# Moving SBUF tile addresses: an arena on a 128-byte boundary, feature tiles 1040 and 1088 bytes apart

## The chip, the cores and the metric

The kernel runs on one core of one Trainium2 chip. The metric is the device time of one execution in microseconds (us), given as the median of several executions. SBUF is the on-chip memory with 128 partitions; an address here is a byte offset within a partition, and it is the same in all 128.

## The reference

The program takes 256 tokens of width 1024 through two networks in float32.

The first has two layers. A layer is a SwiGLU feed-forward (`x += 0.5 * (silu(h @ w_gate) * (h @ w_up)) @ w_down`, hidden width 2816), a mixer (a projection of width about 7300, a gated spatial unit, an RWKV-7 recurrence over time, two gated projections and an output projection), and another SwiGLU feed-forward.

The second has two layers over the tokens and, in its first layer, over 256 context tokens as well: RMS norm with a scale and shift from a conditioning vector, attention (differential in the first layer, neighbourhood attention with a bias in the second), and a feed-forward with a three-tap convolution over positions between its up- and down-projection (hidden width 2816). A last RMS norm gives the output.

What bears on the change is only this: nearly all the arithmetic is products `h @ W`, where `h` has 256 rows and `W` is a large weight matrix.

## The kernel before

**Products.** A product is done in float32r, a 4-byte format of less precision. To come near float32 each operand is split in two: a high part (rounded to float32r) and a low part (the rest). Three matmuls replace one: high x high, high feature x low weight, low feature x high weight.

The weights are the moving operand. They come from HBM as a stream of 371 units of 128 x 2048 float32 (1 MB). SyncE loads a unit into `raw` (2 slots), ScalarE writes `w_hi` (line 1147, 4 slots), VectorE subtracts and writes `w_lo` (line 1668, 4 slots), and TensorE reads both. The features are the stationary operand, stored by feature: a tile `[128, KT, T]` holds K tiles of 256 tokens, and one weight load takes 128 of the tokens, 512 bytes in every partition. `HA_hi`/`HA_lo` are the main feature tiles (8 K tiles each); `HB_hi`/`HB_lo` hold a second stream or the recurrence's output (8 K tiles); `FT_hi`/`FT_lo` hold the hidden features of the feed-forwards (22 K tiles).

`block_wide` multiplies one feature tile set with two units. Its inner part is `unit_wide`; each `mm` is one weight load and one matmul of 512 columns, both recorded at line 481:

```
for k in range(4):
    for t in range(tiles):
        a  = h_hi[:, 4 * part + k, P * t:P * t + P]
        al = h_lo[:, 4 * part + k, P * t:P * t + P]
        mm(acc[:, t, 0:width], a,  w_hi[:, s, cols_], ...)
        mm(acc[:, t, 0:width], a,  w_lo[:, s, cols_], ...)
        mm(acc[:, t, 0:width], al, w_hi[:, s, cols_], ...)
```

So a unit is 24 matmuls. `down_part` does the same for the down-projections with `FT_hi` and `FT_lo`.

**Who writes the features.** ScalarE writes the high part and VectorE the low part. With the per-feature gain (the SwiGLU blocks and the mixer) ScalarE does it at line 1184 and VectorE at lines 1739 and 1740, 24 times each for `HA_hi` and `HA_lo`; the plain features are written at lines 1220 and 1707, those with modulation at lines 1212 and 2161.

**Addresses.** `sb` hands out addresses in a partition one after another, rounded up to 32 bytes; a list of fixed tiles comes first, and then an arena whose tiles overlap in time, each at a fixed offset of whole or half KB. The first free byte is 16,481, so `base`, its next multiple of 64, is 16,512, which is 129 x 128. From there: `raw` 16,384 bytes, `w_hi` and `w_lo` 32,768 each, `X` 8,192. This gives

- `w_hi` at 32,896, `w_lo` at 65,664: both multiples of 128; each matmul's 512 columns start a multiple of 2048 bytes further on,
- `HA_hi` at 106,624 and `HA_lo` at 114,816: multiples of 128, K tiles 1024 bytes apart,
- the arena at 132,064, which is 96 past a multiple of 128 (the small tiles before it add up so). `FT_hi`, `FT_lo`, `HB_hi`, `HB_lo` and all working tiles lie in it, K tiles 1024 apart, so each starts 96 past a multiple of 128.

Of the kernel before, what the change touches and what calls it, by code (L numbers as in the profile page):

```python
# [17 lines left out]
F32 = mybir.dt.float32  # L18
F32R = mybir.dt.float32r
ACT = mybir.ActivationFunctionType  # L20
ALU = mybir.AluOpType
AX = mybir.AxisListType

P = 128
D = 1024
T = 256
NT = T // P
KT = D // P
# [179 lines left out]
def build(nc, wstream, wada, vecs, cols, consts, x_in, ctx_in, mus, lora, lort, wst, convw, cc, lam,  # L208
          toe, rope, window, out, mod_scr, vfirst_scr):
    ctx = ExitStack()  # L210
    with ctx:
        top = nc.sbuf_base
        base = (top + 63) // 64 * 64
        place = {"at": base}

        def sb(name, shape, dt=F32, at=None):
            size = 4 * int(np.prod(shape[1:]))
            if at is None:
                at = place["at"]
                place["at"] += (size + 31) // 32 * 32  # L220
            assert at + size <= nc.sbuf_usable_end, (name, at + size)
            return nc.alloc_sbuf_tensor_at(name, list(shape), dt, offset=at)
# [6 lines left out]
        w_lo = sb("w_lo", [P, SPLIT, UNIT], F32R)  # L229
        ADW = sb("ADW", [P, ADA_SLOTS, UNIT], at=ring)  # L230
        X = sb("X", [P, NT, D])
        HA_hi, HA_lo = sb("HA_hi", [P, KT, T], F32R), sb("HA_lo", [P, KT, T], F32R)
        K_ = sb("K_", [P, NCONST])
        COL = sb("COL", [P, NCOL])
        SS = sb("SS", [P, 32])
# [6 lines left out]
        MODS = sb("MODS", [P, 2, 2, KT, 2])  # L242
        CB = sb("CB", [P, KT, 32])
        GT = sb("GT", [P, 2, 2, 2, KT])
        arena = place["at"]
        KB = 1024

        def ar(name, kib, shape, dt=F32):
            return sb(name, shape, dt, at=arena + int(kib * KB))
# [6 lines left out]
        TF = ar("TF", 72, [P, 2, 512])  # L256
# [873 lines left out]
        def _(act):  # L1130
# [8 lines left out]
            def split(n):  # L1139

                for _ in range(min(n, NUNITS - e.u)):
                    (unit, land), s = arrival(e.u), e.u % SPLIT
                    act.wait_ge(sem[land], c.next(land, 16))
                    if e.u >= SPLIT:
                        act.wait_ge(sem["unit_done"], e.turn() + (e.u + 1 - SPLIT))
                    w = UNIT if c.i is not None else unit_width(e.u)
                    act.activation(w_hi[:, s, 0:w], unit[:, 0:w], ACT.Copy).then_inc(sem["hi_ready"], 1)  # L1147
                    e.u += 1
# [24 lines left out]
            def root(n, dst=None, at=0):  # L1173

                act.wait_ge(sem["rs_pre"], c.next("rs_pre"))
                act.activation(RS[:, at:at + n] if dst is None else dst, RS[:, at:at + n], ACT.Sqrt) \
                    .then_inc(sem["rs_ready"], 1)

            def raw_features(late=2):

                e.skip_turns(4)
                for g in range(KT // 2):
                    act.wait_ge(sem["tf_ready"], c.next("tf_ready"))
                    act.activation(HA_hi[:, 2 * g:2 * g + 2, :].rearrange("p k n -> p (k n)"), TF[:, g % 2, :],
                                   ACT.Copy).then_inc(sem["hi_feat"], 1)
                    if g == 1:
                        split(late)
                act.wait_ge(sem["x_half"], c.next("x_half", 2))
                for t in range(NT):
                    last = act.activation(XN[:, t, :], X[:, t, :], ACT.Square, accum_out=SS[:, t:t + 1])  # L1190
                last.then_inc(sem["ss_ready"], 1)
                root(2, dst=RN)
                act.drain()
# [34 lines left out]

            def swiglu(first=False, last=False):
                raw_features(1 if first else 2)  # L1230
                if first:
                    split(2)
# [88 lines left out]

            def mixer(l):
                raw_features()
                w = SHIFT[l] - 3 * D
                split(1)
# [327 lines left out]
        def _(dve):  # L1653
# [18 lines left out]
            tt, ts, stt = dve.tensor_tensor, dve.tensor_scalar, dve.scalar_tensor_tensor  # L1672
# [44 lines left out]
            def features_scaled(hi, lo, scaled, rest, groups=range(KT // 2)):  # L1717

                def low(g):
                    dve.wait_ge(sem["hi_feat"], c.next("hi_feat"))  # L1720
                    rest(g).then_inc(sem["feat_ready"], 1)

                for g in groups:
                    dve.wait_ge(sem["tp_ready"], c.next("tp_ready"))
                    bank = e.bank()
                    for k in range(2):
                        last = scaled(TF[:, g % 2, T * k:T * k + T], bank[:, T * k:T * k + T], 2 * g + k)
                    last.then_inc(sem["tf_ready"], 1)
                    dve.drain().then_inc(e.tp_free(), 1)
                    if g > groups[0]:  # L1730
                        low(g - 1)
                        dve.drain()
                low(groups[-1])
                dve.drain()

            def raw_half(gain, h):

                features_scaled(
                    HA_hi, HA_lo, lambda dst, src, f: ts(dst, src, COL[:, gain + f:gain + f + 1], None, ALU.mult),
                    lambda g: tt(HA_lo[:, 2 * g:2 * g + 2, :].rearrange("p k n -> p (k n)"), TF[:, g % 2, :],  # L1740
                                 HA_hi[:, 2 * g:2 * g + 2, :].rearrange("p k n -> p (k n)").bitcast(F32),
                                 ALU.subtract), (2 * h, 2 * h + 1))

            def raw_features(gain, residual=None, narrow=False):

                for h in range(2):
                    if residual:
                        residual(h)
                    if narrow and h:
                        split(2)  # L1750
                    raw_half(gain, h)
                    if h == 0 and not residual:
                        split(1)
                if residual:
                    if not narrow:
                        split(2)
                else:
                    lam_sums()
                dve.wait_ge(sem["ss_ready"], c.next("ss_ready"))
                rates(2, D, NORM_EPS)  # L1760
                dve.wait_ge(sem["rs_ready"], c.next("rs_ready"))
# [954 lines left out]
```

## Time and profile before

| | |
|---|---|
| median of 3 executions | 2729.52 us |
| the three executions | 2731.38, 2729.52, 2718.10 us |
| span of the profiled execution | 2721.0 us |
| mean granted TensorE clock, as a share of full | 0.987 |
| TensorE matmul, busy | 2608.7 us (96%) |
| VectorE, busy | 1688.3 us (62%) |
| ScalarE, busy | 1391.1 us (51%) |
| DMA, mean | 174 GB/s |

The span runs from the first to the last instruction of one execution; no separate time of that execution is listed, and the three timed executions lie between 2.9 us below the span and 10.4 us above it. Matmuls overlap in the records (one is shown as some 390 ns long while the next begins 227 ns after it), so what a matmul costs is read from the distance between the starts of two of them, which the text calls the spacing, and not from its duration.

### The profile page before, as it was taken

The page shows a single profiled execution, that of the slowest core. Times are in us where ns is not written, and L with a number is a line of the kernel's source. Part 1 is how long each engine was busy: PE and PEld are TensorE (multiplying, and loading weights), DVE is VectorE, ACT ScalarE, POOL GpSimd, SP SyncE. Part 2 cuts the span into 40 slices and gives each one's busy share as a digit, 9 for nine tenths or more (in the row PEclk, how much of TensorE's full clock was granted, in tenths as well). Part 3 has the DMA queues.
Part 4 walks back from the last instruction along what each step waited for, and adds up shares of the span by engine and source line. Part 5 has one row for each costly group of instructions (what it writes and reads, how often), then busy time and mean ns, then how long its engine had stood idle before and what let it go on. Part 6 is the DMA issues. An engine that isn't in the chain of part 4 may idle for free.

```text
span 2721.0 us, 45474 instructions
## 1 busy us (share of the span) xinstructions
PE 2608.7 (96%) x18123; PEld 2089.3 (77%) x18123; DVE 1688.3 (62%) x1913; ACT 1391.1 (51%) x1633; POOL 81.0 (3%) x113
## 2 busy tenths in 40 slices
PE   7999989999999999989999999989999999998998
PEld 6887567888888886568878878757888887876886
DVE  5545646855555546657665555687776776455675
ACT  4434434634445434334545444575774764465673
POOL 0002000000000001001000000000000000011000
PEclk9999999999999999999999999999999999989999
DMA  5547743544444459444544544304445444523453
GB/s 209 190 177 237 268 153 124 202 184 180 187 175 185 185 180 326 168 169 160 197 172 185 187 169 174 150 1 156 172 185 193 161 185 173 197 93 106 155 185 124
DMA packets 77707, 474.79 MB, mean 174 GB/s; under 512 B 9358, under 2 KB 13564, under 8 KB 27248
## 3 DMA queue, kind: packets, MB, share of 16 engines
q1 hardware_dynamic: 64656, 437.42, 43.6%
q0 software_dynamic: 8288, 30.93, 3.4%
q10 hardware_dynamic: 4608, 4.20, 0.6%
q8 instruction: 120, 1.97, 0.3%
q14 instruction: 35, 0.29, 0.0%
HBM read 463.81 MB, written 2.13 MB: 171 GB/s over the span
## 4 chain that ended last, share of the span: by engine, by line
PE 78%; DMA 10%; DVE 6%; ACT 3%; issue 1%; DVEq 1%; ACTq 0%; POOL 0%; SPq 0%; POOLq 0%
PE ACC L481 70%; DMA ADW<-wada 5%; DMA raw<-wstream 3%; PE TP L557 3%; PE MM L481 2%; DVE w_lo L1668 2%; ACT w_hi L1147 1%; PE TP L481 1%; PE TP L959 1%; DMA BIAS<-toe 0%; DMA PREV<-V 0%; DVE ST L2205 0%; DMA COL<-cols 0%; DVE PR L2217 0%; ACT XX L1303 0%
## 5 line engine op out<-in xcount | busy, mean ns | idle before, releaser
L1668 DVE TENSOR_TENSOR w_lo<-raw,w_hi 128x2048 fp32r<-128x2048 f32 (+2 forms) x371 | 836.2, 2273 | 369.5 <-ACT w_hi L1147 355.0
L1147 ACT ACTIVATE w_hi<-raw 128x2048 fp32r<-128x2048 f32 (+2 forms) x371 | 699.6, 1904 | 393.2 <-DMA raw<-wstream 306.7
L481 PE MATMUL ACC<-w_hi,HA_hi 128*128 128x512 f32 (+1 forms) x2032 | 800.7, 394 | 12.6 <-DVE w_lo L1668 6.9
L481 PE MATMUL ACC<-w_hi,HA_lo 128*128 128x512 f32 (+1 forms) x2032 | 792.0, 390 | 0.1
L481 PE MATMUL ACC<-w_lo,HA_hi 128*128 128x512 f32 (+1 forms) x2032 | 790.7, 389 | 0.0
L481 PEld LDWEIGHTS ACC<-w_hi,HA_hi 128*128 128x128 f32 x2032 | 383.5, 189 | 92.9 <-issue 12.8
L481 PEld LDWEIGHTS ACC<-w_hi,HA_lo 128*128 128x128 f32 x2032 | 383.1, 189 | 80.5 <-issue 0.3
L481 PEld LDWEIGHTS ACC<-w_lo,HA_hi 128*128 128x128 f32 x2032 | 383.9, 189 | 75.8
L481 PE MATMUL ACC<-w_hi,FT_hi 128*128 128x512 f32 x616 | 246.1, 399 | 0.0
L481 PE MATMUL ACC<-w_hi,FT_lo 128*128 128x512 f32 x616 | 244.2, 396 | 0.0
L481 PE MATMUL ACC<-w_lo,FT_hi 128*128 128x512 f32 x616 | 244.1, 396 | 0.0
L1238 ACT ACTIVATE HID<-ACC,ST 128x256 f32<-128x256 f32 x88 | 37.0, 472 | 221.6 <-PE ACC L481 221.6
L1774 DVE SCALAR_TENSOR_TENSOR HID<-ACC,ST,HID 128x256 f32<-128x256 f32 x88 | 38.6, 480 | 168.1 <-ACT HID L1238 168.1
L481 PEld LDWEIGHTS ACC<-w_hi,FT_lo 128*128 128x128 f32 x616 | 116.0, 188 | 28.2
L481 PEld LDWEIGHTS ACC<-w_lo,FT_hi 128*128 128x128 f32 x616 | 116.1, 189 | 27.2
L481 PEld LDWEIGHTS ACC<-w_hi,FT_hi 128*128 128x128 f32 x616 | 116.0, 188 | 27.2
L481 PE MATMUL ACC<-w_hi,HB_hi 128*128 128x512 f32 x320 | 128.2, 401 | 0.0
L481 PE MATMUL ACC<-w_hi,HB_lo 128*128 128x512 f32 x320 | 126.8, 396 | 0.0
L481 PE MATMUL ACC<-w_lo,HB_hi 128*128 128x512 f32 x320 | 126.8, 396 | 0.0
L2400 DVE SCALAR_TENSOR_TENSOR CV<-TP,CW,CV 128x255 f32<-128x255 f32 x132 | 57.7, 478 | 68.9 <-ACT CV L1595 58.8
L481 PEld LDWEIGHTS MM<-VV,AT 128*128 128x128 f32 x448 | 58.3, 205 | 36.3 <-issue 29.5
L481 PE MATMUL MM<-VV,AT 128*128 128x64 f32 (+1 forms) x448 | 66.0, 297 | 6.9 <-ACT AT L1485 5.3
(340 smaller groups left out, 2832.0 us busy)
## 6 DMA issues: line engine op xcount, KB each, us to landing
raw<-wstream SPq DMA_DIRECT2D x367, 1024.0 KB, 4.8
ADW<-wada SPq DMA_DIRECT2D x56, 512.0 KB, 3.7
ADW<-wada SPq DMA_DIRECT2D x20, 1024.0 KB, 14.8
BC<-vecs POOLq DMA_DIRECT2D x14, 512.0 KB, 5.9
BIAS<-toe ACTq DMA_DIRECT2D x32, 128.0 KB, 2.8
BC<-mod_scr POOLq DMA_DIRECT2D x6, 512.0 KB, 5.0
MU<-mus POOLq DMA_DIRECT2D x2, 1280.0 KB, 11.3
WA<-lora POOLq DMA_DIRECT2D x2, 1024.0 KB, 10.4
```

The source lines that it names most:

```text
L481: return pe.matmul(*a, skip_group_check=True, **k)
L557: last = pe.transpose(bank[:, (NT * k + t) * P:(NT * k + t + 1) * P], src[:, t, (k0 + k) * P:(k0 + k + 1) * P], ident())
L959: last = pe.transpose(TP[st["tp"] % 2][:, P * k:P * k + P], (PRB if heads_ == 2 else PR)[:, n % 2, hb, P * k:P * k + P], ident())
L1147: act.activation(w_hi[:, s, 0:w], unit[:, 0:w], ACT.Copy).then_inc(sem["hi_ready"], 1)
L1238: last = act.activation(HID[:, b % 2, t, :], acc[:, t, 0:256], ACT.Silu, scale=RN[:, t:t + 1])
L1668: dve.tensor_tensor(w_lo[:, s, 0:w], unit[:, 0:w], w_hi[:, s, 0:w].bitcast(F32), ALU.subtract).then_inc(sem["lo_ready"], 1)
L1774: last = stt(h, acc[:, t, 256:512], RN[:, t:t + 1], h, ALU.mult, ALU.mult)
L2400: stt(y[:, 1:T], u[:, 0:T - 1], CW[:, 0, col], y[:, 1:T], ALU.mult, ALU.add)
```

## The change

The arena begins on the next multiple of 128. The K tiles of `HA_hi` are 1040 bytes apart (4 float32 of padding each) and those of `HA_lo` 1088 (16 float32 of padding), and `HA_lo` starts on a multiple of 128. The two instructions that wrote or read two K tiles as one run of 512 (lines 1184 and 1740) get them as two runs of 256.

```diff
-        HA_hi, HA_lo = sb("HA_hi", [P, KT, T], F32R), sb("HA_lo", [P, KT, T], F32R)
+        HA_hi = sb("HA_hi", [P, KT, T + 4], F32R)[:, :, 0:T]
+        place["at"] = (place["at"] + 127) // 128 * 128
+        HA_lo = sb("HA_lo", [P, KT, T + 16], F32R)[:, :, 0:T]
...
-        arena = place["at"]
+        arena = (place["at"] + 127) // 128 * 128
...
-                    act.activation(HA_hi[:, 2 * g:2 * g + 2, :].rearrange("p k n -> p (k n)"), TF[:, g % 2, :],
+                    act.activation(HA_hi[:, 2 * g:2 * g + 2, :], TF[:, g % 2, :].rearrange("p (k n) -> p k n", n=T),
...
-                    lambda g: tt(HA_lo[:, 2 * g:2 * g + 2, :].rearrange("p k n -> p (k n)"), TF[:, g % 2, :],
-                                 HA_hi[:, 2 * g:2 * g + 2, :].rearrange("p k n -> p (k n)").bitcast(F32),
-                                 ALU.subtract), (2 * h, 2 * h + 1))
+                    lambda g: tt(HA_lo[:, 2 * g:2 * g + 2, :], TF[:, g % 2, :].rearrange("p (k n) -> p k n", n=T),
+                                 HA_hi[:, 2 * g:2 * g + 2, :].bitcast(F32), ALU.subtract), (2 * h, 2 * h + 1))
```

The addresses that follow: `HA_hi` stays at 106,624 and its K tile k starts 16k bytes past a multiple of 128 (0, 16, ... 112). `HA_lo` starts at 114,944, a multiple of 128, and its K tiles start 0 past it for even k and 64 past it for odd k. The small tiles move by 640 bytes. The arena starts at 132,736, a multiple of 128, and so do all K tiles of `FT` and `HB`. `w_hi`, `w_lo` and `X` do not move.

## Rows read from the trace of the kernel before

**Rows 1.** The page: busy time by engine, and the chain that ended last.

```profile
PE 2608.7 (96%) x18123; PEld 2089.3 (77%) x18123; DVE 1688.3 (62%) x1913; ACT 1391.1 (51%) x1633; POOL 81.0 (3%) x113
...
PE ACC L481 70%; DMA ADW<-wada 5%; DMA raw<-wstream 3%; PE TP L557 3%; PE MM L481 2%; DVE w_lo L1668 2%; ACT w_hi L1147 1%; PE TP L481 1%; PE TP L959 1%; DMA BIAS<-toe 0%; DMA PREV<-V 0%; DVE ST L2205 0%; DMA COL<-cols 0%; DVE PR L2217 0%; ACT XX L1303 0%
```

**Rows 2.** Groups by shape: count, busy us, mean ns, idle time before and releaser.

```profile
L481 PE MATMUL ACC<-w_hi,HA_hi 128*128 128x512 f32 x2000 | 792.0, 396 | 12.6 <-DVE w_lo L1668 6.9 <-DVE HA_lo L1740 5.7
L481 PE MATMUL ACC<-w_hi,HA_lo 128*128 128x512 f32 x2000 | 783.1, 392 | 0.1
L481 PE MATMUL ACC<-w_lo,HA_hi 128*128 128x512 f32 x2000 | 781.9, 391 | 0.0
...
L481 PE MATMUL ACC<-w_hi,FT_hi 128*128 128x512 f32 x616 | 246.1, 399 | 0.0
L481 PE MATMUL ACC<-w_hi,FT_lo 128*128 128x512 f32 x616 | 244.2, 396 | 0.0
...
L481 PE MATMUL ACC<-w_hi,HB_hi 128*128 128x512 f32 x320 | 128.2, 401 | 0.0
L481 PE MATMUL ACC<-w_hi,HB_lo 128*128 128x512 f32 x320 | 126.8, 396 | 0.0
```

**Rows 3.** Timeline of PE, HA features: start us, length us; first and last of 93 matmuls.

```profile
1678.10 0.40 PE L481 MATMUL ACC<-w_hi,HA_hi 128*128 128x512 f32 x1
...
1698.96 0.39 PE L481 MATMUL ACC<-w_hi,HA_lo 128*128 128x512 f32 x1
```

**Rows 4.** The same, HB features (96 matmuls), then FT features (47 matmuls).

```profile
1601.66 0.40 PE L481 MATMUL ACC<-w_hi,HB_hi 128*128 128x512 f32 x1
...
1623.92 0.40 PE L481 MATMUL ACC<-w_hi,HB_lo 128*128 128x512 f32 x1
...
755.20 0.39 PE L481 MATMUL ACC<-w_hi,FT_hi 128*128 128x512 f32 x1
...
765.98 0.39 PE L481 MATMUL ACC<-w_lo,FT_hi 128*128 128x512 f32 x1
```

**Rows 5.** Timeline of PE after a pause, HA features.

```profile
265.15 0.63 PE L481 MATMUL ACC<-w_hi,HA_lo 128*128 128x512 f32 x1
265.58 0.63 PE L481 MATMUL ACC<-w_hi,HA_hi 128*128 128x512 f32 x1
266.00 0.63 PE L481 MATMUL ACC<-w_lo,HA_hi 128*128 128x512 f32 x1
266.43 0.63 PE L481 MATMUL ACC<-w_hi,HA_lo 128*128 128x512 f32 x1
```

**Rows 6.** Four stretches: us, PE busy (count), granted clock, DMA share, GB/s.

```profile
264.80:266.80 2.00, 2.00 (x6) 0.50 0.81 231
1677.63:1698.74 21.11, 21.11 (x95) 1.00 0.45 168
1601.66:1623.69 22.03, 22.03 (x96) 1.00 0.39 142
755.20:765.51 10.31, 10.31 (x46) 1.00 0.60 231
```

**Rows 7.** Groups of the weight stream, and its DMA (KB, median us to landing).

```profile
L1668 DVE TENSOR_TENSOR w_lo<-raw,w_hi 128x2048 fp32r<-128x2048 f32 x367 | 833.3, 2290 | 369.2 <-ACT w_hi L1147 355.0 <-issue 10.7
...
L1147 ACT ACTIVATE w_hi<-raw 128x2048 fp32r<-128x2048 f32 x367 | 696.8, 1918 | 392.9 <-DMA raw<-wstream 306.7 <-PE ACC L481 79.6 <-issue 6.1
...
raw<-wstream SPq DMA_DIRECT2D x367, 1024.0 KB, 4.8
```

**Rows 8.** Feature writers by tile: ns min/median/max, first and last start, forms.

```profile
L1220 ACT ACTIVATE HB_hi<-TP x16: 577/591/600, 509.7 to 1389.2; 128x512 fp32r<-128x512 f32 x16
L1707 DVE TENSOR_TENSOR HB_lo<-TP,HB_hi x16: 683/692/693, 512.0 to 1390.1; 128x512 fp32r<-128x512 f32 x16
...
L1184 ACT ACTIVATE HA_hi<-TF x24: 612/633/637, 14.7 to 1415.7; 128x512 fp32r<-128x512 f32 x24
L1740 DVE TENSOR_TENSOR HA_lo<-TF,HA_hi x24: 691/693/694, 15.8 to 1416.6; 128x512 fp32r<-128x512 f32 x24
L1220 ACT ACTIVATE HA_hi<-TP x12: 592/598/601, 556.3 to 2484.4; 128x512 fp32r<-128x512 f32 x12
L1707 DVE TENSOR_TENSOR HA_lo<-TP,HA_hi x12: 684/691/694, 558.3 to 2485.0; 128x512 fp32r<-128x512 f32 x12
```

## The prediction, made before the changed kernel ran

> **What bounds the kernel.** I read the page's busy times and its chain first: TensorE is busy for 96% of the span, and 70% of the span lies in the chain as matmuls of line 481 into ACC, against 8% for the two weight DMAs and 3% for the split of the weights [rows 1]. Then the groups by shape: the matmuls of HA (6000 of full width, in three groups of 2000) were idle before for 12.7 us in all, those of FT (3 x 616 = 1848) and HB (3 x 320 = 960) for none [rows 2]. So in most of the kernel the end moves one for one with the spacing of the matmuls, and what matters is whether an address changes that spacing. The timeline answers. For HA, 92 spacings take 1698.96 - 1678.10 = 20.86 us, 226.7 ns each [rows 3]. For HB, 95 take 22.26 us, 234.3 ns each, and for FT 46 take 10.78 us, also 234.3 ns [rows 4]. The granted clock is 1.00 in all three stretches [rows 6], the shape is the same, the moving operand is the same w_hi and w_lo, and the order of the loop differs between HB and FT but not between HA and HB. What is left is where the features lie: HA starts on a multiple of 128, the arena 96 past one. That costs 7.6 ns a matmul.
>
> There is room below 226.7 too. After a pause, at a granted clock of 0.50, three spacings take 1.28 us, 426.7 ns each [rows 5, 6]; that is 512 columns at the 1.2 GHz level. At the 2.4 GHz level the columns alone need half, 213.3 ns. So each HA matmul pays 13.4 ns and each HB or FT matmul 21.0 ns beyond its columns, and only at full clock, where the moving stream runs twice as fast against the load of the next weights.
>
> **The arena, term A.** All K tiles of HB and FT come to the alignment that HA has now, with w_hi and w_lo unmoved, so I take HA's spacing: 1848 + 960 = 2808 matmuls by 7.6 ns is 21.3 us less. The smaller bound comes from the groups' mean lengths, 399 to 391 or 396 to 392, some 4 ns, which would be 11 us; the spacing is the better measure because it adds up to the span. Would the weight stream follow? A unit of 24 matmuls goes from 5.62 us to 5.44. The stream already keeps that pace in the HA stages, where TensorE waits 6.9 us for w_lo over 2000 matmuls of a group [rows 2]. With two raw slots one unit needs (4.8 + 1.92 + 2.29) / 2 = 4.5 us [rows 7]. So A passes through: -21 us.
>
> **The K tiles of HA, term B.** There are 4000 loads from HA_hi, 500 for each k, and 2000 from HA_lo, 1000 for even and 1000 for odd k. Their starts past a multiple of 128 become 16k for high, 0 or 64 for low. The trace has a price at 0 (226.7) and at 96 (234.3) and for no other start. High k = 0 and low even k keep 226.7. High k = 6 is at 96: 500 x 7.6 = +3.8 us. The other six high K tiles (3000 loads) and the odd low ones (1000) are unknown. Their floor is the columns alone, 213.3 ns; their ceiling from a row is 234.3. All at the floor: 4000 x -13.4 = -53.6, with k = 6 about -50 us. All at the ceiling: 4000 x 7.6 + 3.8 = +34 us. Nothing in the trace ranks the six starts, so I take the middle, 223.8 ns: 4000 x -2.9 = -11.6, with k = 6 a net of -8 us. At the floor a unit takes 5.12 us, still above the stream's 4.5, so even that gain would not be eaten by w_lo.
>
> I weigh this against the memory's rules. The trace shows two starts, both multiples of 16 bytes, with spacings 7.6 ns apart [rows 3, 4]. The Trainium skill, "SBUF — State Buffer", says in its section on who interferes with whom that TensorE has two independent read ports, one for the moving operand and one for the weights, and that it never waits on anyone, and under port swizzle that what costs is crossing into a new 16-byte line. By these rules no start in this change would cost more than another, A and B would both be 0, and the time 2729.5. The trace disagrees for the pair it can show, so I give the rules little weight for A and some for B.
>
> **The writers, term C.** ScalarE and VectorE write HB at 96 and HA at 0 in the same time: 591 against 598 ns at line 1220, 692 against 691 at line 1707 [rows 8], so moving the arena or the tiles costs them nothing. Lines 1184 and 1740 now handle two runs of 256 with a gap. Line 1220 already gets its tile as two rows of 256 and takes 598 ns where line 1184 takes 633. I take 0. The bound above is that each takes twice as long: 24 x 0.63 + 24 x 0.69 = 32 us of work. Of that only what TensorE waits for counts; it now waits 5.7 us for HA_lo in all [rows 2], and twice that is 6 us more, within the range. No instruction, DMA or wait is added or moved, and nothing is put behind another on any queue.
>
> **Sum.** -21 - 8 + 0 = -29 us. The profiled execution's span of 2721.0 would become 2692; against the median, 2729.5 - 29 = 2700 us. No difference under 0.5%, 13.6 us, can be told from no change.
>
> **Rivals.**
> 1. *The stagger buys much.* Weights and moving operand all start on multiples of 128 now, so both streams may meet at the same place again and again: the spacing repeats to the nanosecond. If most of the six new starts avoid it, HA falls toward 213 to 218 ns: 4000 by 9 to 13 ns is 36 to 54 us, with A 2655 to 2685. For it speaks that 13.4 ns of it is to be had, and that at half clock nothing of it is seen; against it that the only start off 128 in the trace is worse.
> 2. *The stagger does nothing* and A holds: 2729.5 - 21 = 2708.
> 3. *The stagger spoils what the arena gains.* If a start off 128 costs what 96 costs, HA pays up to +34 us, and with A the time is 2716 to 2743, no change. For it: the one row at such a start.
> 4. *Slower.* One mechanism: because high and low loads now alternate between different starts, HA never settles in its even 226.7 and every one of the 6000 pays more than FT does now. From 238 ns on in the mean (6000 x 11.3 = +68 us, less 21) the time is above 2776; the point from which it decides is +5.8 ns a matmul, 35 us, where the sum passes +13.6. For it: 16 and 48 are finer offsets than 96, which may cut more pieces off a load than 96 does. Against: half the low loads and an eighth of the high ones stay where they were.
> 5. *Nothing moves, the arena included*, because the 7.6 ns belong to something else that HB and FT share: 2729.5. Against: HB and FT have no other thing in common that HA lacks.
>
> **How the numbers follow.** My forecast's own band, 2685 to 2716, holds rival 2 too and gets 0.45 (0.17 of it rival 2). Rival 1, below 2685: 0.23. Rivals 3 and 5, from 2716 to 2743: 0.23. Rival 4, above: 0.09. Faster by over 0.5% is 0.45 + 0.23 = 0.68; the same 0.23; slower 0.09. The range runs from 2660, near B's floor with A (-71 gives 2658), to 2740, near B's ceiling with A (+13 gives 2743). The forecast alone would reach from 2685 to 2716.
>
> **What would show it.** A is right if, with the granted clock at 1.00, FT and HB are spaced at 226.7 ns with no wait for w_lo before them; wrong if they stay at 234.3. B shows in the spacing of HA over a run of some 90 matmuls: below 226.7 the stagger helps, and within a unit one sees for which k. If the spacing alternates irregularly around 231 to 238, rival 3 or 4 holds. If the spacing falls and the span does not, the groups of HA will show idle time before them released by w_lo. The prediction fails most simply if the mean spacing of HA is outside 219 to 229 ns.

## The result: no faster, 0.25% slower

The changed kernel takes 2732.41 us (median of 15, 2725.41 to 2737.24) against 2727.93 us for the kernel before in the same rounds; the ratio is 1.0025, 95% interval 1.0015 to 1.0036. Forecast was 2700 us. By the bound of 0.5% this is no change, but it is two changes that cancel: the arena (the feature tiles FT and HB) gave what was forecast of it, and the main feature tiles HA took more than that.

The page of the changed kernel, busy times and spans of the chain; the lines to hold beside them are in [rows 1]:

```profile
PE 2613.5 (96%) x18123; PEld 2087.4 (76%) x18123; DVE 1688.5 (62%) x1913; ACT 1388.7 (51%) x1633; POOL 80.6 (3%) x113
...
PE ACC L483 71%; DMA raw<-wstream 4%; PE TP L559 3%; PE MM L483 3%; DVE w_lo L1670 2%; PE TP L483 2%; ACT w_hi L1149 2%; DMA ADW<-wada 1%; DMA BIAS<-toe 1%; ACT XX L1305 1%; DVE ST L2232 0%; DMA PREV<-V 0%; DVE TM L1969 0%; DVE ST L2206 0%; DVE PR L2218 0%
```

Its groups by shape (count, busy us, mean ns, idle before; L483 is L481 of before):

```profile
L483 PE MATMUL ACC<-w_hi,HA_hi 128*128 128x512 f32 x2000 | 803.8, 402 | 13.9 <-DVE w_lo L1670 7.2 <-DVE HA_lo L1742 6.6
L483 PE MATMUL ACC<-w_hi,HA_lo 128*128 128x512 f32 x2000 | 792.3, 396 | 0.1
L483 PE MATMUL ACC<-w_hi,FT_hi 128*128 128x512 f32 x616 | 241.8, 393 | 0.0
L483 PE MATMUL ACC<-w_hi,HB_hi 128*128 128x512 f32 x320 | 126.1, 394 | 0.0
```

Beside [rows 2], the mean length of the HA matmuls rose (396 to 402, 392 to 396) and that of FT and HB fell (399 to 393, 401 to 394). TensorE's waits hardly changed: 14.0 us before the HA matmuls against 12.7. So the reader looks for the difference in the spacing. Timeline of PE in the changed kernel, first and last of 93 matmuls each, at a granted clock of full speed:

```profile
1617.46 0.39 PE L483 MATMUL ACC<-w_hi,HB_hi 128*128 128x512 f32 x1
...
1638.31 0.39 PE L483 MATMUL ACC<-w_hi,HB_lo 128*128 128x512 f32 x1
...
1691.11 0.39 PE L483 MATMUL ACC<-w_hi,HA_hi 128*128 128x512 f32 x1
...
1712.46 0.39 PE L483 MATMUL ACC<-w_hi,HA_lo 128*128 128x512 f32 x1
```

HB: 20.85 / 92 = 226.6 ns, where [rows 4] gave 234.3. HA: 21.35 / 92 = 232.1 ns, where [rows 3] gave 226.7. With the counts of the prediction, 2808 x -7.6 = -21 and 6000 x +5.4 = +32, +11 us in all. The span grew from 2721.0 to 2732.0, by 11.0; the ratio, which rests on 15 executions of each kernel, says 7.

### The profile page after: what moved, and what is told of

The parts are those of the page before. It is cut to its first block, busy times and chain, and to the rows that moved or that the text cites. A ratio compares the mean times of both kernels' runs of the same rounds, so it can differ in the third digit from the quotient of the medians.

```text
span 2732.0 us, 45474 instructions
## 1 busy us (share of the span) xinstructions
PE 2613.5 (96%) x18123; PEld 2087.4 (76%) x18123; DVE 1688.5 (62%) x1913; ACT 1388.7 (51%) x1633; POOL 80.6 (3%) x113
## 4 chain that ended last, share of the span: by engine, by line
PE 79%; DVE 7%; DMA 6%; ACT 4%; issue 2%; DVEq 1%; ACTq 0%; POOL 0%; SPq 0%; POOLq 0%
PE ACC L483 71%; DMA raw<-wstream 4%; PE TP L559 3%; PE MM L483 3%; DVE w_lo L1670 2%; PE TP L483 2%; ACT w_hi L1149 2%; DMA ADW<-wada 1%; DMA BIAS<-toe 1%; ACT XX L1305 1%; DVE ST L2232 0%; DMA PREV<-V 0%; DVE TM L1969 0%; DVE ST L2206 0%; DVE PR L2218 0%
## 5 line engine op out<-in xcount | busy, mean ns | idle before, releaser
L483 PE MATMUL ACC<-w_hi,HA_hi 128*128 128x512 f32 (+1 forms) x2032 | 812.5, 400 | 13.9 <-DVE w_lo L1670 7.2
L483 PE MATMUL ACC<-w_hi,HA_lo 128*128 128x512 f32 (+1 forms) x2032 | 801.0, 394 | 0.1
L483 PE MATMUL ACC<-w_lo,HA_hi 128*128 128x512 f32 (+1 forms) x2032 | 798.4, 393 | 0.0
L483 PEld LDWEIGHTS ACC<-w_hi,HA_hi 128*128 128x128 f32 x2032 | 384.5, 189 | 100.1 <-issue 13.7
L483 PEld LDWEIGHTS ACC<-w_hi,HA_lo 128*128 128x128 f32 x2032 | 385.5, 190 | 91.6 <-issue 0.3
L483 PEld LDWEIGHTS ACC<-w_lo,HA_hi 128*128 128x128 f32 x2032 | 384.0, 189 | 84.5
L483 PE MATMUL ACC<-w_hi,FT_hi 128*128 128x512 f32 x616 | 241.8, 393 | 0.0
L483 PE MATMUL ACC<-w_hi,FT_lo 128*128 128x512 f32 x616 | 239.9, 389 | 0.0
L483 PE MATMUL ACC<-w_lo,FT_hi 128*128 128x512 f32 x616 | 239.8, 389 | 0.0
L483 PEld LDWEIGHTS ACC<-w_hi,FT_lo 128*128 128x128 f32 x616 | 115.6, 188 | 24.0
L483 PEld LDWEIGHTS ACC<-w_lo,FT_hi 128*128 128x128 f32 x616 | 115.7, 188 | 23.4
L483 PEld LDWEIGHTS ACC<-w_hi,FT_hi 128*128 128x128 f32 x616 | 115.7, 188 | 23.3
L483 PE MATMUL ACC<-w_hi,HB_hi 128*128 128x512 f32 x320 | 126.1, 394 | 0.0
L483 PE MATMUL ACC<-w_lo,HB_hi 128*128 128x512 f32 x320 | 124.7, 390 | 0.0
L483 PE MATMUL ACC<-w_hi,HB_lo 128*128 128x512 f32 x320 | 124.6, 389 | 0.0
L483 PEld LDWEIGHTS MM<-VV,AT 128*128 128x128 f32 x448 | 54.5, 194 | 35.3 <-issue 24.3
L483 PEld LDWEIGHTS ACC<-w_hi,HB_hi 128*128 128x128 f32 x320 | 60.1, 188 | 12.8 <-DVE w_lo L1670 0.8
```

The lines of the kernel that those rows point to most:

```text
L483: return pe.matmul(*a, skip_group_check=True, **k)
```

## The experiments

All times of a version are beside the kernel before on the same chip (2725.9 to 2728.2 us median). A version with a ratio was executed 4 to 12 times; one with a time alone was executed once, and since single executions of the kernel before lie between 2717 and 2740 us, it is judged by its spacing. "Spacing" is read as above, from two starts 92 matmuls apart in one unbroken run, at full clock. An edit is shown against the kernel before; all keep the writers' two runs of 256.

The granted clock is not the same in all executions. Matmuls at half clock are spaced at 426.7 ns [rows 5, 6], about twice as far, so each thousandth of mean granted clock is worth some 2.7 us of these 2728. Where that matters, a time is multiplied by its mean granted clock; this is an estimate of how long it would be at full clock throughout, called "at full clock" below. The kernel before comes to 2689 to 2691 us.

**The two parts apart.** First the arena alone, moved to the next multiple of 128 (address 132,096):

```diff
-        arena = place["at"]
+        arena = (place["at"] + 127) // 128 * 128
```

> Only the arena is on a 128-byte boundary; the K tiles of HA stay 1024 bytes apart, their writers keep the form with two runs of 256. The changed kernel showed FT and HB at 226.7 ns and HA near 232 ns instead of 226.7. If the two parts add up, this kernel keeps HA at 226.7 ns and gives 2808 x 7.6 = 21 us back: near 2707 us, ratio 0.992. The rival is that less time in the FT and HB matmuls is eaten by waits for the weight stream or for the writers (the changed kernel gained less than its parts suggest): then the ratio lies above 0.996 though the spacings are 226.7, and waits in front of the HA and FT matmuls have grown.

Measured: ratio 0.9976 (0.9965 to 0.9987), 2721.2 us. Not the 0.992 expected, and not by waits, which did not grow (11.9 us before the HA matmuls). HA is at 226.6 ns, but HB is not:

```profile
1604.71 0.40 PE L485 MATMUL ACC<-w_hi,HB_hi 128*128 128x512 f32 x1
...
1626.09 0.39 PE L485 MATMUL ACC<-w_hi,HB_lo 128*128 128x512 f32 x1
```

21.38 / 92 = 232.4 ns. 2808 x 1.9 = 5 us, 0.2%, is what the ratio says. A multiple of 128 alone is thus not what HA had and the arena lacked.

Then the strides alone:

```diff
+        HA_hi = sb("HA_hi", [P, KT, T + 4], F32R)[:, :, 0:T]
+        place["at"] = (place["at"] + 127) // 128 * 128
+        HA_lo = sb("HA_lo", [P, KT, T + 16], F32R)[:, :, 0:T]
...
-        arena = place["at"]
+        arena = (place["at"] + 127) // 128 * 128 - 32
```

> Only the K tiles of HA are 1040 and 1088 bytes apart; the arena stays 96 past a multiple of 128. If the parts add up: HA near 232 ns, 6000 x 5.4 = 32 us more, less what little the waits give back, so 2755 to 2762 us, ratio 1.010 to 1.012, FT and HB at 234.3 ns. If the loss in HA came from something that the shifted arena does, HA is back at 226.7 ns and the ratio is 1.00.

Measured: ratio 1.0077 (1.0057 to 1.0097), 2746.9 us; HA at 232.1 ns. The arena moved with the padding to 132,704, and HB was at 233.3. The ratio is below the 1.010 to 1.012 expected. The spacings give 32 us for HA less 3 for the arena, +29; measured are 19 to 21. Most of what lacks is the clock: 0.989 in the mean of its four executions against 0.987 beside them, and at full clock it is 26 us longer. The loss is in HA's new places. This edit also holds the later start of HA_lo, which is tried by itself further down.

**Which address counts.** Two versions were meant to put all K tiles of HA at one start: HA_hi and HA_lo with 1024 between K tiles, their beginnings 16 or 48 past a multiple of 128, and the arena 32 or 64 past one.

```diff
+        HA_hi = sb("HA_hi", [P, KT * T + 4], F32R)[:, 4:4 + KT * T].rearrange("p (k n) -> p k n", n=T)
+        place["at"] = (place["at"] + 127) // 128 * 128
+        HA_lo = sb("HA_lo", [P, KT * T + 4], F32R)[:, 4:4 + KT * T].rearrange("p (k n) -> p k n", n=T)
...
+        arena = (place["at"] + 127) // 128 * 128 + 32
```

> All K tiles of HA start 16 bytes past a multiple of 128, 1024 apart, and the arena 32 past one. Theory one, a price for each start: 16 is one of the starts that the changed HA used, whose mean was 232 ns, so HA is at about 230 to 234 ns, and FT and HB at 32 are at some price of their own. Theory two, the even 226.7 ns is a state into which a row of equal starts settles and which mixed starts break: then a uniform start of 16 settles too, at 226.7 ns or at another value that repeats, and FT and HB at 32 likewise. Under theory two the uniform 96 of before should have settled, and it did not (231 to 238 in turn), so theory two also needs the start to be right for it.

> All K tiles of HA start 48 past a multiple of 128, the arena 64 past one. If what counts repeats every 64 bytes, FT and HB at 64 are at 226.7 ns as at 0; if it repeats every 128 bytes, they are elsewhere, between 213 and 238. HA at 48: theory one says 230 to 234 ns; theory two as in the run with 16 and 32.

Measured: 2747.7 and 2731.4 us; HB at 233.4 and 228.8. The rounding between the two tiles put HA_lo 128 further on than HA_hi (16 and 144 bytes from the weights' start modulo 512 in the first version, 48 and 176 in the second), so they did not have one start after all, and neither of the two theories is decided by them. HA of the second was at 231.1 ns. The first nevertheless shows what a price per start cannot explain. Timeline of HA in that kernel, a stretch at 480 us (88 matmuls) and one at 1704 us (93):

```profile
479.62 0.39 PE L485 MATMUL ACC<-w_hi,HA_hi 128*128 128x512 f32 x1
...
499.92 0.40 PE L485 MATMUL ACC<-w_hi,HA_hi 128*128 128x512 f32 x1
```

```profile
1704.44 0.39 PE L485 MATMUL ACC<-w_hi,HA_hi 128*128 128x512 f32 x1
...
1725.29 0.39 PE L485 MATMUL ACC<-w_hi,HA_lo 128*128 128x512 f32 x1
```

20.30 us over 87 spacings is 233.3 ns, 20.85 us over 92 is 226.6, over the same tiles and slots at the same addresses and at a granted clock of 1.00 in both. A third value, 235.7 ns, holds from 43.30 us on (46 spacings in 10.84 us). So the text speaks of a rhythm: a run of matmuls keeps one of a few spacings, and the addresses alone do not say which. What picks it is not shown.

**The distance from the weights.** w_hi and w_lo begin 128 past a multiple of 512, and so do HA before and the arena of the changed kernel. With the arena there and HA untouched:

```diff
+        place["at"] += (128 - place["at"]) % 512
         arena = place["at"]
```

> The run with the arena alone on a multiple of 128 (it lay at 132,096, a multiple of 512) kept FT and HB at 232.4 ns, while the changed kernel, whose arena lies at 132,736, 128 past a multiple of 512 like HA and like the weights, showed 226.7. New theory: what counts is the distance of the features' start from the weights' start, modulo 512. Here the arena is at 132,224, 128 past a multiple of 512, and HA is untouched: FT, HB and HA all at 226.7 ns, 2808 x 7.6 = 21 us less, ratio 0.992 to 0.994. Rival: the modulus is larger (1024), which the two arenas tell apart (132,736 is 640 past a multiple of 1024, 132,224 is 128 past one); or the gain in the changed kernel came from something in HA's new places: then FT and HB are not at 226.7 ns and the ratio is above 0.996.

Measured: ratio 0.9932 (0.9906 to 0.9958), 2706.8 us, span 2705.8; HB and HA both at 226.6 ns. Term A, in full, and the best version found. The rival with a modulus of 1024 cannot be judged by these two arenas: the two loads of a K tile lie 512 bytes apart, so each version has both places. Against it speaks that the two do not differ: in the version with the arena alone moved, FT's spacings have the same mean, 232.4 ns, whether the first or the second 128 tokens are used.

The counter-proof moves the weights and leaves the features' addresses modulo 512 where they were:

```diff
+        place["at"] += (256 - place["at"]) % 512
         ring = place["at"]
         w_hi = sb("w_hi", [P, SPLIT, UNIT], F32R)
...
+        place["at"] += (128 - place["at"]) % 512
         HA_hi = sb("HA_hi", [P, KT, T], F32R)
+        place["at"] += (128 - place["at"]) % 512
         HA_lo = sb("HA_lo", [P, KT, T], F32R)
...
+        place["at"] += (128 - place["at"]) % 512
         arena = place["at"]
```

> w_hi and w_lo lie 128 bytes later, at 256 past a multiple of 512; HA and the arena stay at 128 past one, where both showed 226.7 ns. If the distance between features and weights counts, the distance is now 384 modulo 512 for all of them, the one at which FT and HB showed 232.4 ns in the run with the arena alone on a multiple of 128: 8700 matmuls by 5.7 ns is 50 us more than the run with everything at 128, so near 2755 us, ratio 1.010 or a little more. If the features' own address counts, everything stays at 226.7 ns and the ratio is 0.993.

Measured: ratio 1.0059 (1.0041 to 1.0077), 2743.8 us, span 2748.1 against 2705.8 for the run before it. The features' own addresses are at 128 past a multiple of 512 in both, and yet HA is slow:

```profile
1698.09 0.39 PE L486 MATMUL ACC<-w_hi,HA_hi 128*128 128x512 f32 x1
...
1719.46 0.39 PE L486 MATMUL ACC<-w_hi,HA_lo 128*128 128x512 f32 x1
```

21.37 / 92 = 232.3 ns, the value of distance 384, as expected. The features' own address modulo 512 does not explain this, and the distance does; the weights were moved by this one amount only. The ratio came out at 1.006 and not 1.010. The clock is part of it: 0.989 in the mean against 0.986 beside it, and at full clock this version is 26 us longer than the kernel before. The span, at nearly the same clock (0.987 and 0.986), is 42 us above that of the run with everything at 128, where 50 were expected.

**The other distances.** Three versions, executed once each, with HA at one distance and the arena at another:

```diff
+        place["at"] += (192 - place["at"]) % 512
         HA_hi = sb("HA_hi", [P, KT, T], F32R)
+        place["at"] += (192 - place["at"]) % 512
         HA_lo = sb("HA_lo", [P, KT, T], F32R)
...
+        place["at"] += (384 - place["at"]) % 512
         arena = place["at"]
```

> Distances from the weights' start modulo 512: HA 64, FT and HB 256. A price for each distance: so far 0 gives 226.7, 160 gives 233.4, 192 gives 229.1, 352 gives 234.3, 384 gives 232.4, 480 gives 233.3. If distance 0 is the best there is, both are above 226.7. If some distance lets the two streams miss each other, it comes toward 213.3.

> Distances modulo 512: HA 128, FT and HB 448. As the run before: above 226.7 if distance 0 is the best. HA at a uniform 128 also tells whether it was the mixing of 0 and 128 that cost 4 ns where only the low tiles had been moved, or the distance 128 itself: mixing predicts that a uniform 128 is nearer to 226.7 than the 231.2 of the mixture, the price of the distance predicts more than 231.2.

> Distances modulo 512: HA 32, FT and HB 96. Above 226.7 if distance 0 is the best; between 229 and 235 like the others.

Measured: 2741.6, 2736.8 and 2752.1 us. Timeline of the first, HB at distance 256 and HA at 64:

```profile
1617.71 0.39 PE L485 MATMUL ACC<-w_hi,HB_hi 128*128 128x512 f32 x1
...
1638.56 0.40 PE L485 MATMUL ACC<-w_hi,HB_lo 128*128 128x512 f32 x1
...
1691.48 0.39 PE L485 MATMUL ACC<-w_hi,HA_hi 128*128 128x512 f32 x1
...
1712.95 0.40 PE L485 MATMUL ACC<-w_hi,HA_lo 128*128 128x512 f32 x1
```

226.6 and 233.4 ns. So the expectation that only distance 0 modulo 512 gives 226.7 failed: 256 does too. Read in the same way from all runs in which a tile set has one distance:

| distance modulo 256 | distances tried (modulo 512) | spacing, ns |
|---|---|---|
| 0 | 0, 256 | 226.6, 226.6 |
| 32 | 32 | 233.3 |
| 64 | 64 | 233.4 |
| 96 | 352, 96 | 234.3, 234.2 |
| 128 | 384, 128 | 232.4, 232.4 |
| 160 | 160 | 233.4 |
| 192 | 192, 448 | 228.8, 228.9 |
| 224 | 480 | 233.3 |

In the four rows in which both halves of 512 were tried they agree within 0.1 ns, so the pattern repeats every 256 bytes, and 0 is the best of the eight. None comes near the 213.3 ns of the columns alone. At half clock the distance made no difference: the spacing of HA was 426.6 to 426.7 ns in the mean of each trace in which HA has one distance (0, 32, 64, 128 or 384). HA at distance 64 (the first of the three versions), a granted clock of 0.50:

```profile
265.22 0.63 PE L485 MATMUL ACC<-w_lo,HA_hi 128*128 128x512 f32 x1
...
270.34 0.63 PE L485 MATMUL ACC<-w_lo,HA_hi 128*128 128x512 f32 x1
```

Twelve spacings take 5.12 us, 426.7 ns each, as at distance 0 [rows 5].

**Which part of HA's layout.** The arena at distance 0 in all three; each was executed once.

Only the start of HA_lo, 128 later, which in the change comes from HA_hi's own padding (8 x 16 bytes):

```diff
         HA_hi = sb("HA_hi", [P, KT, T], F32R)
+        place["at"] += (256 - place["at"]) % 512
         HA_lo = sb("HA_lo", [P, KT, T], F32R)
```

> Arena 128 past a multiple of 512; both HA tiles with K tiles 1024 apart, and HA_lo begins 128 bytes later than before, at 114,944, as in the changed kernel. So only the step of 128 that the rounding put between high and low is tried. Theory of the distance modulo 512: low loads now lie at another distance than high ones, so HA leaves 226.7 ns: 229 to 233, and some 15 to 35 us are lost against the run with the arena alone at this place. Rival, that the two strides alone slow HA: HA stays at 226.7 ns.

Only the high stride (`T + 4`, HA_lo at distance 0), and only the low one (`T + 16`, from distance 0):

> Arena 128 past a multiple of 512, HA_lo 1024 apart and at distance 0 from the weights modulo 512, HA_hi 1040 apart. Theory: the high tiles' eight starts (0 to 112) make HA leave 226.7 ns, 230 to 233 ns. Rival: the high stride is harmless and the step or the stride of the low tiles does it all: 226.7 ns.

> Arena 128 past a multiple of 512, HA_hi 1024 apart, HA_lo 1088 apart from the same start as before. The low tiles' starts are 0, 64, ... 448 past the weights' modulo 512. Theory: a third of the loads at changing distances is enough to break the even 226.7 ns: 229 to 232 ns. Rival of a price per load: only a third of the loads can cost more, by at most 7.6 ns each, so the mean is at most 229.2 ns, and the matmuls that run while high tiles are loaded stay at 226.7.

Measured, against 226.6 ns and 2706.8 us with none of them: HA_lo's start 231.1 ns and 2728.6 us; high stride 231.4 and 2723.9; low stride 229.6 and 2725.0. Their clocks were 0.989, 0.991 and 0.986; at full clock they are 26, 27 and 14 us above the version with none, and the spacings give 27, 29 and 18. Alone they bring 4.5, 4.8 and 3.0 ns, together 5.4, so they do not add. The first shows this most plainly. PE timeline, HA_hi at distance 0, HA_lo at 128:

```profile
1700.40 0.39 PE L485 MATMUL ACC<-w_hi,HA_hi 128*128 128x512 f32 x1
1700.63 0.40 PE L485 MATMUL ACC<-w_lo,HA_hi 128*128 128x512 f32 x1
1700.86 0.40 PE L485 MATMUL ACC<-w_hi,HA_lo 128*128 128x512 f32 x1
1701.10 0.39 PE L485 MATMUL ACC<-w_hi,HA_hi 128*128 128x512 f32 x1
...
1702.48 0.39 PE L485 MATMUL ACC<-w_hi,HA_hi 128*128 128x512 f32 x1
1702.71 0.40 PE L485 MATMUL ACC<-w_lo,HA_hi 128*128 128x512 f32 x1
1702.94 0.40 PE L485 MATMUL ACC<-w_hi,HA_lo 128*128 128x512 f32 x1
1703.18 0.39 PE L485 MATMUL ACC<-w_hi,HA_hi 128*128 128x512 f32 x1
```

While a matmul runs, the weights of the next are loaded. In the four triples from 1700.40 on, the first spacing, with a high tile loaded, is 227 ns in the mean; the second, with the low tile at 128 loaded, is 232; the third, with a high tile at distance 0 loaded again, is 235. Over the whole trace they are 227, 232 and 234. The slowest of the three is the one in which the load is from the good distance. A price per load would give (2 x 226.6 + 232.4) / 3 = 228.5 in the mean; measured is 231.1. The spacing after the odd load is slow as well. But distance 128 itself costs too: with all of HA at 128 the spacing was 232.4, above that of the mixture.

The rival of the low stride, at most 229.2 ns, is passed by the mean of 229.6, by little. Its other sign decides: high tiles were to stay at 226.7, and over the whole trace the spacings in which one is loaded are 229.7 and 231.4 ns in the mean, and that with a low tile 228.8.

## Why the prediction was wrong, by its own steps

- **Where the time is set** held. In the five versions with a ratio (the changed kernel, the arena alone, the strides alone, everything at 128, the weights moved) the spacings of HA, HB and FT give +11, -5, +29, -21 and +29 us, and at full clock the versions are +7, -6, +26, -18 and +26 us from the kernel before. None of them waits more for w_lo than the changed kernel, whose groups show 7.2 us where it was 6.9.
- **Term A, the arena**: forecast -21 us, and 2808 x 7.6 ns were there (226.6 ns; the arena at distance 0 alone gives a ratio of 0.9932, -19 us). The size was right and the reason wrong. The prediction put it down to a start on a multiple of 128; such a start alone gave 1.9 ns of the 7.6. The changed kernel got the rest by luck: the 640 bytes of padding happened to carry the arena to a multiple of 256 away from the weights.
- **Term B, the K tiles of HA, is the step that failed**: forecast -8 us, measured +32 by spacing (232.1 ns against a forecast mean near 225.4, and outside the 219 to 229 that the prediction named as its limit). Two things in it were wrong. It took the unknown starts at the middle between the columns alone and the worst row, 223.8 ns; every distance tried but 0 lies between 228.8 and 234.3, so the floor that it averaged with was not reachable by any of them. And it reckoned a price for each load: high k = 0 and low even k were to keep 226.7. They do not: with low tiles at another distance, spacings with a high tile at distance 0 loaded took 235 ns. It also gave no price to the step by which HA_lo begins 128 bytes later, since that is again a multiple of 128; the step alone costs 4.5 ns.
- **Term C, the writers**: 0, and it is. ScalarE's and VectorE's times over two runs with a gap are those of [rows 8], 633 and 693 ns:

```profile
L1186 ACT ACTIVATE HA_hi<-TF x24: 611/632/638, 12.9 to 1431.7; 128x512 fp32r<-128x512 f32 x24
...
L1742 DVE TENSOR_TENSOR HA_lo<-TF,HA_hi x24: 691/693/696, 13.9 to 1432.6; 128x512 fp32r<-128x512 f32 x24
```

- **The rivals.** Rival 3, the stagger spoils what the arena gains, 2716 to 2743 us, is what happened in time and in size; it had the better argument of the trace for it, the one row off HA's start, and was given less than the forecast, which rested on a middle that nothing supported. Its mechanism, a price for each start off 128, is not what the runs show. Rival 4's, that unlike starts in turn keep all of HA from its even 226.7, fits them better; only its price was too high (+5.4 ns, not above 5.8). In rival 1 the sum slipped: 36 us less with A gives 2672, not 2685.

What stays open is why 256 bytes of distance close the circle and why 192 is better than 160 or 224. At 192 the three spacings of a triple are unlike though all tiles have one distance: 231.5, 229.4 and 225.9 ns in the mean of FT, at distance 448. Why the granted clock was higher in some versions is open too. Starts of HA at odd multiples of 16 were tried only together with a low tile 128 further on, so their own rhythm is not known.

## What to carry to other kernels

Where TensorE sets the time with a weight load for each matmul, read the spacing of its matmuls per tile, not their length: here one layout ran 3% faster than another with the same instructions (226.6 against 234.3 ns). Only float32r with 512 columns a matmul was tried. For such a kernel, give stationary and moving tiles start addresses whose distance is a multiple of 256 bytes, and all stationary tiles used in turn the same distance; padding between tiles to "spread" them did harm here. And when an address changes, list all addresses that move with it, since in this case most of the gain and part of the loss came from places that tiles took only because something ahead of them grew.

## What the runs showed of the hardware that was not expected

- The spacing of 512-column matmuls at full clock depends on the distance between the features' and the weights' addresses modulo 256: 226.6 ns at 0, 228.8 at 192, 232.4 to 234.3 at the other multiples of 32. At half clock it does not: 426.7 ns at distance 0 [rows 5] and at 64. The Trainium skill, "SBUF — State Buffer", section on who interferes with whom, gives TensorE two independent read ports and has it wait on nobody; these runs disagree, by up to 7.7 ns in 234.3.
- The cost does not add up load by load. With low tiles at distance 128 and high tiles at 0 the mean was 231.1 ns, where prices per load give 228.5. Where high and low tiles lay at 16 and 144, the same tiles ran at 233.3 ns in one stretch and at 226.6 in another of one execution.
